# Decoder layer, last part: the rows of the last two experts stay on chip and are summed by fp32 matrices of gates on TensorE

## The reference

```python
def _moe(x, w_router, b_router, w_e_gate, w_e_up, w_e_down):
    ...
    vals, idx = lax.top_k(jnp.where(in_group, probs, -1.0), TOP_K)
    wts = vals / jnp.sum(vals, -1, keepdims=True)
    gate = jnp.sum(jax.nn.one_hot(idx, N_EXPERTS, dtype=jnp.float32) * wts[..., None], axis=1)
    h = jax.nn.silu(jnp.einsum('nd,edf->nef', xt, w_e_gate)) * jnp.einsum('nd,edf->nef', xt, w_e_up)
    h = h * gate[..., None].astype(h.dtype)
    return jnp.einsum('nef,efd->nd', h, w_e_down).reshape(B, T, D)
...
x = _layer_norm(ALPHA * x + _moe(x, w_router, b_router, w_e_gate, w_e_up, w_e_down), ln2_g, ln2_b)
```

## Time and profile before

| what | us |
|---|---|
| median of 3 runs (898.61 to 899.36) | 899.3 |
| the profiled execution, its own time | 900.57 |
| its span in the trace, first to last instruction | 899.3 |
| TensorE busy in the span | 867.6 (96%) |
| VectorE / ScalarE / GpSimd busy | 360.5 / 206.3 / 85.6 |
| end of the last expert's matmuls in the trace | 861.9 |
| last output store issued | 893.0 |
| mean granted clock of TensorE, share of full speed | 0.990 |

### The profile page before, as it was taken

The page is one execution under the profiler, slowest core; times in us unless marked ns, Lnnn a source line. Parts: engine busy times, 40 slices in busy tenths (PEclk is TensorE's granted clock), DMA queues, the critical chain, the costliest instruction groups (busy, mean ns, idle before and its releaser), DMA issues.

```text
span 899.3 us, 20975 instructions
## 1 busy us (share of the span) xinstructions
PE 867.6 (96%) x9437; PEld 710.4 (79%) x9437; DVE 360.5 (40%) x749; ACT 206.3 (23%) x313; POOL 85.6 (10%) x89
## 2 busy tenths in 40 slices
PE   7999999999999999999999999999999999999964
PEld 6999888898989999999999988666666566565631
DVE  5653645736575372233232555722311211111146
ACT  4521141311422332322221201231111111111112
POOL 1210000000000001001101021400001000100053
PEclk9999999999999999999999999999999999999987
DMA  9895171492816043222221923699999999999566
GB/s 323 268 286 152 48 264 65 146 313 64 280 48 211 1 156 93 84 67 87 94 95 47 378 102 151 243 371 400 401 404 405 398 410 411 406 404 424 215 210 125
DMA packets 85374, 203.47 MB, mean 226 GB/s; under 512 B 4237, under 2 KB 57189, under 8 KB 76472
## 3 DMA queue, kind: packets, MB, share of 16 engines
q1 hardware_dynamic: 78216, 177.17, 53.5%
q0 software_dynamic: 7088, 25.26, 9.1%
HBM read 172.58 MB, written 32.06 MB: 228 GB/s over the span
## 4 chain that ended last, share of the span: by engine, by line
PE 91%; DMA 4%; DVE 2%; ACT 1%; issue 1%; POOL 0%; SPq 0%; DVEq 0%; POOLq 0%
PE psum L2159 18%; PE psum L465 17%; PE psum L467 17%; PE psum L466 16%; PE psum L2173 9%; PE psum L1863 2%; DMA xg<-x_rows,idx_i 2%; PE psum L1873 2%; PE psum L2146 2%; PE psum L1902 1%; PE psum L2105 1%; PE psum L2072 1%; DMA ya_rows<-y_slots,dest_i 1%; DMA xn<-in_x_prompt_dram 1%; PE psum L1888 1%; PE psum L2037 1%
## 5 line engine op out<-in xcount | busy, mean ns | idle before, releaser
L465 PE MATMUL psum<-x_hi,split_lo 128*128 128x272 f32 x704 | 208.9, 297 | 2.0 <-DVE pbl L1427 1.2
L467 PE MATMUL psum<-x_hi,split_hi 128*128 128x272 f32 x704 | 202.3, 287 | 0.0
L466 PE MATMUL psum<-x_lo,split_hi 128*128 128x272 f32 x704 | 202.1, 287 | 0.0
L2159 PE MATMUL psum<-set,xt 128*32 128x256 f32 x3072 | 169.1, 380 | 0.0
L2159 PEld LDWEIGHTS psum<-set,xt 128*32 128x32 f32 x3072 | 98.2, 110 | 65.7 <-issue 2.4
L465 PEld LDWEIGHTS psum<-x_hi,split_lo 128*128 128x128 f32 x704 | 132.6, 188 | 7.3 <-issue 2.7
L466 PEld LDWEIGHTS psum<-x_lo,split_hi 128*128 128x128 f32 x704 | 132.8, 189 | 1.4 <-issue 1.0
L467 PEld LDWEIGHTS psum<-x_hi,split_hi 128*128 128x128 f32 x704 | 132.6, 188 | 0.0
L460 DVE TENSOR_TENSOR split_lo<-raw,split_hi 128x2048 fp32r<-128x2048 f32 x35 | 80.0, 2290 | 113.8 <-ACT split_hi L441 113.3
L2173 PE MATMUL psum<-set,hT 128*32 128x256 f32 x1536 | 86.2, 380 | 1.5 <-DVE ys L1651 1.5
L2173 PEld LDWEIGHTS psum<-set,hT 128*32 128x32 f32 x1536 | 49.0, 110 | 32.8 <-ACT hT L1051 1.7
(11 more groups left out here) (355 smaller groups left out, 1250.3 us busy)
## 6 DMA issues: line engine op xcount, KB each, us to landing
set<-in_w_e_gate_dram SPq DMA_DIRECT2D x32, 1024.0 KB, 18.3
set<-in_w_e_up_dram SPq DMA_DIRECT2D x32, 1024.0 KB, 20.9
set<-in_w_e_down_dram SPq DMA_DIRECT2D x32, 1024.0 KB, 21.2
raw<-in_w_in_dram SPq DMA_DIRECT2D x26, 1024.0 KB, 6.5
cb<-in_state_C_dram SPq DMA_DIRECT2D x8, 1024.0 KB, 7.9
out_dram<-cb SPq DMA_DIRECT2D x8, 1024.0 KB, 5.8
y_slots<-ys POOLq DMA_DIRECT2D x15, 384.0 KB, 7.3
y_slots<-x_hi POOLq DMA_DIRECT2D x3, 1536.0 KB, 14.8
```

The lines of the kernel that those rows point to most:

```text
L465: nc.tensor.matmul(out, a_lo, b_hi, start=first, stop=False)
L466: nc.tensor.matmul(out, a_hi, b_lo, start=False, stop=False)
L467: return nc.tensor.matmul(out, a_hi, b_hi, start=False, stop=last)
L2159: last = mm(gate_up()[32 * b:32 * b + 32, j], xt[:, kk, 32 * mine:32 * mine + 32], w, start=kk == 0 and j != 1, stop=kk == KT - 1 and j > 0)
```

## The change

The change rewrites the end, and prepares it earlier:

- Experts 14 and 15 are not stored to HBM. Their 96 result rows stay in `ys[0]` and `ys[1]`. For both, their rows of `y_slots` are zero: SP writes them by four DMAs near 183 us, GpSimd's one DMA at 49 us is gone.
- The gates of experts 14 and 15 are cut in three bf16 parts and put beside the token numbers in `named` (VectorE, nine small instructions in `choice_gates`). The last `rows_of` multiplies by `named` in place of `tok_bf`; VectorE's `late_slots`, 17 instructions behind turn 4, makes of it `oh14` and `oh15`: 96 slots x 544 tokens in fp32, the gate where a slot belongs to a token, else zero.
- All ten gathers are issued once experts 0 to 13 are stored. Both gated additions, `add_first` and `add_second`, are on VectorE; `diag` and its five ScalarE instructions are gone.
- TensorE sums for each block: identity x `x1`, `oh14` x `ys[0]`, `oh15` x `ys[1]`, all in full fp32 (30 calls of up to 512 columns where there were 20).
- The transposes of expert 15's hidden values stand between the halves of `down(14)`, they are copied to a buffer of their own (`hT_last`), and `down(15)` writes banks 6 and 7. ScalarE copies all of expert 14's result and columns 0 to 767 of expert 15's, VectorE the rest of 15's (three instructions).
- The code for additional blocks moves behind the end, on every engine, and does the sum of all blocks anew if it runs. SP loads the count and branches when all outputs have landed.

```diff
-        pl.wait_ge(ys_out[0], 16 * NE // 2)
-        pl.wait_ge(ys_out[1], 16 * (NE // 2 - 1))
-        pl.wait_ge(dn_done, 2 * NE - 2)
-        for i in range(NT):
-            gather_rows(0, ya, i)
-        pl.wait_ge(last_out, 32)
-        for i in range(NT):
-            gather_rows(1, yb_, i)
+        pl.wait_ge(ys_out[0], 16 * (NE // 2 - 1))
+        pl.wait_ge(ys_out[1], 16 * (NE // 2 - 1))
+        for i in range(NT):
+            gather_rows(0, ya, i)
+        pl.wait_ge(gu_done, 2 * NE - 2)
+        for i in range(NT):
+            gather_rows(1, yb_, i)
...
+                for e in (NE - 2, NE - 1):
+                    for c in (0, 512):
+                        sp.dma_start(y_slots[e * CAP:(e + 1) * CAP, c:c + 512], const("head_sel")[32:32 + CAP, 0:512]
+                                     ).then_inc(zero_out, 16)
...
+        sp.wait_ge(outs, 16 * NT)
+        sp.wait_ge(cp_out, 16 * H)
         sp.wait_ge(xa_ok, 1)
         extra = sp.value_load(ctl[0:1, XTRA:XTRA + 1], min_val=0, max_val=XTRA)
...
+        for i in range(2):
+            add_first(i)
+        add_first(2)
+        add_first(3)
         ve_.wait_ge(ys_out[1], 16 * (NE // 2 - 1))
+        ve_.wait_ge(dn_done, 2 * NE)
+        ve_.wait_ge(yd_ok, NE - 1)
+        for b in range(QB):
+            last = v.tensor_copy(ys[1][b * 32:b * 32 + 32, 768:DM], results_last()[CAP:P, 256 * b:256 * b + 256])
+        last.then_inc(yd_ok, 1)
+        add_second(0)
+        add_second(1)
...
+        stats(0)
+        for i in range(NT):
+            centred(i)
+            if i < 2:
+                add_second(i + 2)
+            if i == 2:
+                add_first(PT)
+                add_second(PT)
+            if i < NT - 1:
+                stats(i + 1)
...
+        def own_rows(i, first=True):
+            r = ROWS[i]
+            pe.wait_ge(xa2_ok, ROWS_AT[i])
+            if i >= PT:
+                pe.wait_ge(pf_ok, i - PT + 1)
+            for b in range(2):
+                mm(summed(i)[0:r, b, :], ident[0:r, 0:r], x1[0:r, i, b * 512:b * 512 + 512], start=first, stop=False)
+
+        def add_late(i, q, first=False):
+            r = ROWS[i]
+            pe.wait_ge(ya_ok, NE - 1 + q)
+            pe.wait_ge(yd_ok, NE - 1 + q)
+            for b in range(2):
+                last = mm(summed(i)[0:r, b, :], late[q][0:CAP, P * i:P * i + r], ys[q][0:CAP, b * 512:b * 512 + 512],
+                          start=first, stop=q == 1)
+            if q:
+                last.then_inc(pc_ok, 1)
+
+        for i in range(2):
+            add_late(i, 0, True)
+        for i in range(2):
+            own_rows(i, False)
+            add_late(i, 1)
+        for i in range(2, NT):
+            own_rows(i)
+            add_late(i, 0)
+            add_late(i, 1)
```

More of the change, by code:

```diff
@@ L297, in build @@
     yb_ = [ybk[:, i, :] for i in range(NT)]
+    hT_last = place("hT_last", [P, QB, P], F32, r_ht + NT * DM * 4)
+    oh15 = place("oh15", [P, N], F32, at_route + DM * 4)
+    late = (oh14, oh15)
     psum = ctx.enter_context(nc.psum_tensor("psum", [P, 8, 512], F32))
@@ L1613, in choice_gates @@
             step(v.tensor_reduce(gates_ab[:, 1, :], lg[:], AX.X, ALU.add))
+            part = lambda k: named[:, :, 1:3, 2 + k:3 + k].rearrange("p i e o -> p i (e o)")
+            v.memset(named[:, :, 0, 2:5], 0.0)
+            numbers = const("tokid").rearrange("p (i q) -> p i q", q=2)
+            for e in range(3):
+                last = v.tensor_copy(named[:, :, e, 0:2], numbers)
+            step(last)
+            step(v.tensor_copy(part(0), gate[:, :, NE - 2:NE]))
+            step(v.tensor_tensor(rest[:], gate[:, :, NE - 2:NE], part(0), ALU.subtract))
+            step(v.tensor_copy(part(1), rest[:]))
+            step(v.tensor_tensor(rest[:], rest[:], part(1), ALU.subtract))
+            step(v.tensor_copy(part(2), rest[:]))
         def extra_blocks():
@@ L1655, in _, with late_slots @@
         choice_gates()
+        def late_slots():
+            found = psum[0:CAP, 7, 96:3 * 96].rearrange("p (e c) -> p e c", c=96)[:, :, 2:5]
+            step(v.tensor_reduce(gslot[0:CAP], found, AX.X, ALU.add))
+            step(v.tensor_copy(tok_f[0:CAP], idx_i[0:CAP, NE - 2:NE]))
+            for i in range(NT):
+                last = v.tensor_scalar(tok_at[0:CAP, :, i:i + 1].rearrange("p e o -> p (e o)"), tok_f[0:CAP],
+                                       float(1 - P * i), None, ALU.add)
+            step(last)
+            for q, oh in enumerate(late):
+                for i in range(NT):
+                    r = ROWS[i]
+                    last = v.tensor_scalar(oh[0:CAP, P * i:P * i + r], const("slot", CAP)[:, 0:r], tok_at[0:CAP, q, i:i + 1],
+                                           gslot[0:CAP, q:q + 1], ALU.is_equal, ALU.mult)
+            step(last)
         def turn(e, odd, y_used=None):
@@ L1672, in _ @@
         turn(4, False, y_used=(ys_out[1], 16))
+        ve_.wait_ge(idx_ok, 6)
+        late_slots()
         with ve_.Fori(2, NE // 2 - 1) as t:
@@ L1677, in _, with step2, add_first @@
             st.end(NE // 2 - 3)
-        turn(NE - 1, True, y_used=(ys_out[0], 16 * (NE // 2 - 1)))
-        ve_.wait_ge(ys_out[1], 16 * (NE // 2 - 1))
-        store_half(1, 2 * NE)
+        tail = Steps(dve_tail)
+        def step2(ins):
+            ve_.wait_ge(dve_tail, tail.mark(ins))
+        def add_first(i):
+            r = ROWS[i]
+            ve_.wait_ge(xal_ok, i + 1)
+            ve_.wait_ge(ya_in[i], 16)
+            v.scalar_tensor_tensor(x1[0:r, i, :], ya[i][0:r], gates_ab[0:r, 0, i:i + 1], x1[0:r, i, :], ALU.mult, ALU.add
+                                   ).then_inc(xa2_ok, 1)
@@ new lines, in add_second @@
+        def add_second(i):
+            r = ROWS[i]
+            ve_.wait_ge(xa2_ok, i + 1 if i < PT else ROWS_AT[PT] - 1)
+            ve_.wait_ge(yb_in[i], 16)
+            v.scalar_tensor_tensor(x1[0:r, i, :], yb_[i][0:r], gates_ab[0:r, 1, i:i + 1], x1[0:r, i, :], ALU.mult, ALU.add
+                                   ).then_inc(xa2_ok, 1)
+        silu(NE - 1)
+        for i in range(2):
+            add_first(i)
+        add_first(2)
+        add_first(3)
+        ve_.wait_ge(ys_out[1], 16 * (NE // 2 - 1))
@@ new lines, in _, with stats @@
+        ve_.wait_ge(dn_done, 2 * NE)
+        ve_.wait_ge(yd_ok, NE - 1)
+        for b in range(QB):
+            last = v.tensor_copy(ys[1][b * 32:b * 32 + 32, 768:DM], results_last()[CAP:P, 256 * b:256 * b + 256])
+        last.then_inc(yd_ok, 1)
+        add_second(0)
+        add_second(1)
+        ve_.wait_ge(ln_in, 48)
+        def stats(i):
+            r = ROWS[i]
+            ve_.wait_ge(pc_ok, i + 1)
+            for q in range(2):
+                last = v.bn_stats(lst[0:r, i, q, :], summed(i)[0:r, q, :])
+            step2(last)
+            step2(v.bn_aggr(hmv[0:r, i, :], lst[0:r, i].rearrange("p q s -> p (q s)")))
+            v.tensor_scalar(hve[0:r, i:i + 1], hmv[0:r, i, 1:2], EPS, None, ALU.add).then_inc(v2_ok, 1)
@@ new lines, in centred @@
+        def centred(i):
+            r = ROWS[i]
+            v.scalar_tensor_tensor(x1[0:r, i, :], summed(i)[0:r].rearrange("p b n -> p (b n)"), hmv[0:r, i, 0:1],
+                                   lng[0:r, :], ALU.subtract, ALU.mult).then_inc(pf_ok, 1)
+        stats(0)
+        for i in range(NT):
+            centred(i)
[6 more added lines that the diff above has]
+                stats(i + 1)
@@ L2161, in up, with down @@
             last.then_inc(gu_done, 1)
-        def down(p, loaded, half):
+        def down(p, loaded, half, hT=hT, results=results):
             pe.wait_ge(set_in[p][4 + half], loaded)
```

195 lines of the change are left out of this document (96 added, 99 removed).

## The result

The changed kernel takes 908.96 us (median of 4 runs, 906.93 to 910.57), the kernel before 899.31: a ratio of 1.0109 (95% interval 1.009 to 1.0129). It is 1.1% slower, clear of the noise, and 6.5 us above the top of the range. Its runs spread over 3.6 us, those of before over 0.8. The profiled execution is the fastest of the four, 906.93 with a span of 905.7.

The account below looks back on a forecast made before the run. TensorE was taken to bound the kernel up to the last expert, then, after rows pass through HBM, VectorE. From the 899.3 us span, -0.7 (sum), -0.6 (landing) and +1.1 (branch) gave -0.2, 899.1 us; range 896.4 to 902.5.

Parts of the forecast that it names:

- Up to 849 us: nothing: Before down(14): the added DMAs and small VectorE instructions were to cost no time, covered by idle times and buffers.
- down(15) 1.5 us earlier: Last expert's down on TensorE: was to end at 860.3 against 861.86, without waiting for copies out of its banks.
- The gathers: hidden: Ten gathers beside the downs: first out at about 846.6, ten out by 859, rows there in time.
- TensorE as the bound of the sum: Final sum: three pairs a block, 5.16 us where 3.44; of 9.5 us gained 8.8 given back, last statistics 888.0.
- The end: Last store and after: landing 5.6 us (before 6.2), 0.6 less; SP's count load and branch, 1.1 more.
- rival A: At the end: the last store lands in 3.6 us, 2.0 less than in the sum, total 897.1; chance 0.20.
- the 5 us that the forecast named as a sign of being wrong: At the end: a landing of the last store under 5 us would show the forecast wrong.
- The rule weighed: Gathers beside VectorE additions: the skill's rule would keep 0.95 us each, profile rows said 1.89; the forecast followed the rows.
- rival B: Gathers late, all stretched by additions to 2.19 us: block 0's sum up to 3.2 us late, total 902.3; chance 0.10.
- Rival C: TensorE's clock falls in the 0.85 us wait ahead of block 2, losing 3.4 us, at most 902.5; chance 0.08.
- The 0.15 for what no row showed: Whole kernel: some 0.15 set aside for what no row of the profile showed.
- the forecast's 0.7 us: Sum at the end: the last store was to be issued at 892.35, a gain of 0.7 us.

Follow-up runs that it names:

- e1: Changed kernel, but all ten gathers of result rows wait until down(15) is done; 913.5 us (1.0165).
- e9: Changed kernel, but its ten gathers also wait for the end of up(15); 907.5 us (1.0088).
- e14: Changed kernel with each of the ten gathers replaced by a plain transfer of as many rows, in table order, issued by GpSimd; 900.1 us (1.0001).
- e18: e3 once more, with more runs; 906.1 us.
- e3: Kernel before with ten additional gathers of 96 rows that nobody reads, issued once expert 13 is stored; 905.7 us.
- e6: e1 with ten gathers of 96 rows that nobody reads in the early place; 925.2 us.
- e5: Changed kernel, gathers early, but the four additions of ya stand behind VectorE's copies of down(15)'s result; 917.7 us (1.0197).
- e8: Changed kernel again without an edit, for a second profile; 912.5 us.
- e11: Changed kernel with 128 additional instructions (waits already met) at the start of TensorE's program; 922.9 us.
- e15: Changed kernel with 63 additional instructions (32 small transposes) at the start of TensorE's code; 909.5 us (1.009).
- e16: Changed kernel with 191 additional instructions (96 small transposes) at the start of TensorE's code; 913.7 us (1.0137).
- e17: Changed kernel with down(15) done four times, three passes in a loop and one written out, gathers from the end of pass 1; 918.3 us.
- e2: e1 with ten plain SyncE transfers of the same number of bytes beside the downs, where the gathers were; 914.9 us (1.0184).
- e7: e1 with four VectorE additions on data at hand beside the downs, no early gather; 914.1 us.
- e10: Changed kernel, but its gathers wait for the first half of down(14); 910.7 us (1.0114).
- e13: Changed kernel with each of the ten gathers replaced by a plain transfer of as many rows, in table order, issued by SyncE; 900.3 us (1.0006).

## Why the prediction was wrong
- **Up to 849 us: nothing.** Right to 0.1 us. From the transposes of expert 1's rows (590.09 before, 591.13 here) to those of expert 14's hidden values (838.26 and 839.38) the kernel before takes 248.17 us and the changed one 248.25, so VectorE's 26 instructions are covered. The other 1.0 us is there at 590 and varies with the run: the changed kernel has 590.31 in e1, 590.21 in e9 and 591.14 in e14, the one before 590.05 in e18 and 590.62 in e3. Nearly all of it is there at TensorE's first product of the projections already, 12.18 us before and 13.32 here, behind its wait for the first data and ahead of everything that the change adds: e1, the changed code too, has 12.25, and e3, the code before, 12.98. So it belongs to the start of a run and not to the change.
- **down(15) 1.5 us earlier.** Right: without gathers beside it, from start to end 11.1 us (forecast 11.0), where before took 12.7 (849.13 to 861.86).
- **The gathers: hidden.** This is the step that failed. I asked whether they come in time, and they did: no own rows waited for one. I did not ask what they do to the engine that they run beside. The gathers of the earlier trace rows ran where TensorE idled or made long calls, and no row had one beside a down; it was set at no cost without one. The trace of before had one gather beside such calls (606.17 and 611.80 us), and it cost nothing, so that row would have agreed with the forecast. What it lacked is ten of them in a row. It costs 4.9 to 11.6 us of the stretch (changed kernel and e6), the clock that falls within the gaps included. Their start was misjudged too: 849.12 and not 846.6 plus the 1.1 of the start, since expert 13's store, issued at 841.8, took 6.8 us to land and not the 5.6 of the earlier trace rows; ten took 14.5 us to issue and not 12.5.
- **TensorE as the bound of the sum.** Right to a few tenths, as e14 shows, which starts 1.1 us late: first statistics 868.59 (forecast 867.3 + 1.1), waits only ahead of block 2 (0.84) and the short block (0.35), last statistics 889.17 (888.0 + 1.1), last store 4.35 us behind them.
- **The end.** The landing was mis-sized: 4.1 us (3.9 in e14), between the forecast's 5.6 and rival A's 3.6, and under the 5 us that the forecast named as a sign of being wrong. SyncE's branch behind it took 1.5, not 1.1. From the last store's issue to the end of the span pass 5.6 us (5.4), where the sum had 6.7. With the start's 1.1 us against it, e14 ends where the forecast has it, 898.9 against 899.1 on the span's scale. That is two misses that cancel, luck for the sum.
- **The rule weighed.** Gathers beside additions took 1.60, 1.75, 1.47 and 1.33 us, in e5 without additions all ten took 0.87 to 1.01: the rows' side held. A gather reads its row numbers (`dest_i`) from SBUF; whether that is why stays open. It gave rival B no weight: of the sum nothing waited for a gather.
- **Rival C** had the clock fall ahead of block 2. That wait, 0.83 us, cost no clock. It fell elsewhere: within the gaps (e5), and in the short block. There the eight records took 5.32 us in the changed kernel, e8, e11, e15, e16 and e17, and 3.62 in e1, e2, e5, e6, e7, e9, e10, e13 and e14. Gaps don't decide it: e17 had none and e9 had 6.9 us of them. What does is open, so the 1.7 us of it are a second loss beside that of the gaps, not shown to be its consequence.
- **The range** ended at 902.5 because no case in it put idle time on TensorE while its data were at hand. The 0.15 for what no row showed had no price; a bound such as half speed beside the gathers, 11 us of work and so 11 us more, would have been near 910.

## What to carry to other kernels
A transfer that is moved beside another engine's densest stretch needs a row of that very pair and in that number, since being on time is only half of hidden and one gather's row says nothing of ten; without such a row the range has to hold the engine's work there at half speed. One run with the transfer made plain, of the same size and from the same queue, tells what the schedule is worth and what the kind of transfer costs. And a step that takes work off HBM but hands the sum half more calls moves the bound and gains next to nothing, as the forecast's 0.7 us said from the profile of before.

## What the hardware showed that I had not expected
- Gathers by indices beside TensorE's dense small calls: 4.9 to 11.6 us lost beside 11.1 us of work, at a step of 0.72 us. Plain transfers from either queue, at up to 424 GB/s, cost nothing. Neither did one gather alone (turn 2 of the kernel before), nor ten in e3 and e18.
- The clock can fall under a busy TensorE: in the short block, 32 columns of weights wide, 0.50 at 892 to 894 us.
- Ten additional gathers of 3.9 MB in the loop cost 18.9 us (span 930.1 against 911.2), twice what the bytes take at the 400 GB/s of the weights.
- 128 wait instructions that are already met keep TensorE busy from 2.85 to 16.66 us in e11, 108 ns each. They cost it 11.5 us and not 13.8 (`down(14)` at 861.74 against 850.24), since without them it waits for its first data until 5.39. 191 small transposes cost 2.3.
